# Loosening two waits and regrouping ScalarE's and VectorE's steps between the gMLP layer and the attention layer

## What is computed

```python
y = gmlp_mixer(rms_norm_2(h, a_pre_g[i]), a_w_in[i], ..., a_w_out[i])   # ends in: return y @ w_out
h = h + rms_norm_2(y, a_post_g[i])
kv_in = rms_norm_2(h, kv_norm_g)
k_shared = (kv_in @ w_k).reshape(...)
v_shared = (kv_in @ w_v).reshape(...)
...
y = swa_mixer(rms_norm_2(h, b_pre_g[j]), k_shared, v_shared, b_w_in[j], b_sinks[j], b_w_out[j])
```

## Time and profile before

| | us |
|---|---|
| median of three runs | 874.07 |
| lowest, highest | 873.93, 875.82 |
| the profiled execution | 875.82 |
| its span in the trace | 874.1 |

### The profile page before, as it was taken

How to read it: one execution, slowest core, us unless ns; L and a number is a source line. 1 busy time by engine, 2 the same in 40 slices (tenths; PEclk the granted TensorE clock), 3 DMA queues, 4 the chain that set the end, 5 groups by cost and what they waited for, 6 DMA issues and landing times.

```text
span 874.1 us, 11938 instructions
## 1 busy us (share of the span) xinstructions
PE 862.1 (99%) x4196; PEld 717.8 (82%) x4196; DVE 571.8 (65%) x924; ACT 389.1 (45%) x834; POOL 487.3 (56%) x544
## 2 busy tenths in 40 slices
PE   8999999999999999999999999999999999999997
PEld 6888888888888788888888888888878888888875
DVE  6125647865997589676766535556987477798624
ACT  4123433423666377555112321112787447667622
POOL 7766555682217922318975048771224997566362
PEclk9999999999999999999999999999999999999999
DMA  7543222453971468994742253525963222112202
GB/s 200 168 122 97 73 75 71 130 132 76 224 233 49 141 147 179 219 230 147 173 116 94 82 184 99 127 88 144 229 156 99 73 96 74 49 49 73 73 1 96
DMA packets 83691, 106.84 MB, mean 122 GB/s; under 512 B 11953, under 2 KB 54449, under 8 KB 83634
## 3 DMA queue, kind: packets, MB, share of 16 engines
q1 hardware_dynamic: 72752, 85.12, 30.5%
q0 software_dynamic: 10880, 20.97, 14.2%
q10 hardware_dynamic: 2, 0.00, 0.0%
HBM read 103.98 MB, written 2.10 MB: 121 GB/s over the span
## 4 chain that ended last, share of the span: by engine, by line
PE 90%; POOL 2%; DMA 2%; ACT 2%; issue 2%; DVE 1%; DVEq 0%; POOLq 0%; SPq 0%; ACTq 0%
PE bank L2221 27%; PE bank L2222 27%; PE bank L2223 27%; PE bank L2465 2%; PE bank L2318 1%; PE bank L2493 1%; PE bank L2438 1%; DMA smC<-in_w_v 1%; POOL wlo L880 1%; PE bank L2488 1%; PE bank L2487 1%; POOL ms L830 1%; DMA raw<-in_a_w_out 1%; DVE wlo L1692 1%; ACT junk L980 1%
## 5 line engine op out<-in xcount | busy, mean ns | idle before, releaser
L880 POOL TENSOR_TENSOR wlo<-raw,whi 128x512 fp32r<-128x512 f32 x180 | 247.6, 1407 | 6.3 <-PE bank L2318 5.2
L871 POOL TENSOR_SCALAR whi<-raw 128x512 fp32r<-128x512 f32 x174 | 123.9, 752 | 168.5 <-PE bank L2223 161.1
L2221 PE MATMUL bank<-actB_hi,whi 128*128 128x512 f32 (+1 forms) x416 | 159.6, 384 | 0.1
L2222 PE MATMUL bank<-actB_lo,whi 128*128 128x512 f32 (+1 forms) x416 | 158.6, 381 | 0.0
L2223 PE MATMUL bank<-actB_hi,wlo 128*128 128x512 f32 (+1 forms) x416 | 158.5, 381 | 0.0
L2221 PE MATMUL bank<-whi,actA_hi 128*128 128x512 f32 x350 | 138.2, 395 | 1.2 <-DVE actA_lo L1517 0.7
L2223 PE MATMUL bank<-whi,actA_lo 128*128 128x512 f32 x350 | 136.4, 390 | 0.0
L2222 PE MATMUL bank<-wlo,actA_hi 128*128 128x512 f32 x350 | 136.3, 389 | 0.0
L2223 PEld LDWEIGHTS bank<-actB_hi,wlo 128*128 128x128 f32 x416 | 78.2, 188 | 15.2
L2221 PEld LDWEIGHTS bank<-actB_hi,whi 128*128 128x128 f32 x416 | 78.3, 188 | 15.1 <-issue 0.6
L2222 PEld LDWEIGHTS bank<-actB_lo,whi 128*128 128x128 f32 x416 | 78.3, 188 | 14.0
(11 more groups left out here) (275 smaller groups left out, 1639.3 us busy)
## 6 DMA issues: line engine op xcount, KB each, us to landing
raw<-in_a_w_in SPq DMA_DIRECT2D x44, 512.0 KB, 4.0
raw<-in_w_in SPq DMA_DIRECT2D x32, 512.0 KB, 3.9
raw<-in_b_w_in SPq DMA_DIRECT2D x16, 512.0 KB, 3.4
raw<-in_a_w_out SPq DMA_DIRECT2D x12, 512.0 KB, 3.5
gain<-in_a_w_out POOLq DMA_DIRECT2D x9, 512.0 KB, 9.3
raw<-in_w_ple_gate SPq DMA_DIRECT2D x8, 512.0 KB, 5.1
gain<-in_a_w_in POOLq DMA_DIRECT2D x8, 512.0 KB, 7.1
raw<-in_a_w_in POOLq DMA_DIRECT2D x8, 512.0 KB, 7.4
```

Source lines behind the costliest of these rows:

```text
L871: pool.tensor_scalar(H, src[:, i * HALF:(i + 1) * HALF], 1.0, 1.0, ALU.mult, ALU.mult).then_inc(w_hi, 1)
L880: ins = pool.tensor_tensor(L, src[:, i * HALF:(i + 1) * HALF], H.bitcast(f32), ALU.subtract)
L2221: M(out_, whi_, xhi_, start=start, stop=False)
L2222: M(out_, whi_, xlo_, start=False, stop=False)
```

## The change

It has no new instructions and takes none away. It drops two waits, and it moves steps on ScalarE and VectorE:

```diff
@@ add_a, on POOL
-                    if n == 13:
-                        pool.wait_ge(raw_in[10 + h], LANDED[UNIT_NO["v5", 0], h])
@@ ScalarE
             scale_two("v5", 0)
             hi_a(10)
+            scale_two("v5", 1)
             hi_a(11)
-            scale_two("v5", 1)
             square_a(2, 1)
...
             hi_a(13, (1,))
+            scale_two("k5", 1)
             h3_out(0)
-            scale_two("k5", 1)
             normed_n(0)
-            hi_k5(0)
             h3_out(1)
             turned_n(0)
             normed_n(1)
             square_a(2, 0)
+            hi_k5(0)
             turned_n(1)
+            square_a(3, 0)
             hi_k5(1)
-            square_a(3, 0)
             h3_out(2)
@@ h3_in, on VectorE
-                if t % 2:
-                    dve.wait_ge(rstd_ready["h3"], t)
@@ VectorE
             part_gain(0, 1)
+            lo_a(13, (0,))
             h3_in(0)
-            for h in range(2):
-                lo_a(13, (h,))
             part_gain(1, 1)
+            lo_a(13, (1,))
             h3_in(1)
...
             lo_two(UNIT_NO["v5", 0], 1)
-            lo_two(UNIT_NO["k5", 0], 0)
             add_kept(6, 1, p03_kept(1), a_out_(3, 0), (c7_made, 42 + 10))
             rest_n(1)
             part_gain(2, 0)
             h3_in(2)
-            lo_two(UNIT_NO["k5", 0], 1)
+            for h in range(2):
+                lo_two(UNIT_NO["k5", 0], h)
             part_gain(3, 0)
             h3_in(3)
```

## The result

The changed kernel takes **878.78 us** (median of 4 executions, 878.43 to 879.38) against 874.05 us before: a ratio of **1.0054, 95% interval 1.0041 to 1.0068**. It is slower by 4.7 us, where the forecast was 874.2 us with a range up to 876.7. The profiled execution, one more than these four, took 878.94 us with a span of 877.2 us.

The account below looks back on a forecast made before the run. TensorE, busy without a break after 680 us, was taken as the bound, with 2.66 us idle ahead. Terms 0 + 0 + 0.55 - 0.94 + 0.7 - 0.15, about +0.15 us on the 874.07 median, gave 874.2 us; range 872.5 to 876.7.

Parts of the forecast that it names:

- part 3: Tile 0 of n: k5's scaling ahead of the squares and VectorE's new order make it 0.55 us later.
- row of 0.84 us: Earlier trace row of a POOL step beside an h3_in, taken as the length of tile 0's held root step.
- part 2: ScalarE scales v5's second half before a11's high halves: price 0, with about 1.0 us of cover.
- cover of v5's landing: VectorE is busy until 642.23, hiding about 1.0 us of a11's delay unless v5's second half lands after 639.5.
- Part 1: POOL's a13 adding loads no longer wait for v5, issuing near 630.0 and 631.2: worth 0, price 0.
- would have to share from about 636 us: v5's second half shares with a13's loads only for its last estimated 0.1 MB, taking 1.7 us, landing at 637 to 639.
- row of 1.86 us: Earlier trace row of tile 0's POOL step at 655.24, which took 0.29 us with VectorE silent.
- Part 6: Tiles 2 and 3: tile 2's root waits until about 671.3; the chain releasing 679.03 comes out at 679.2.
- rival b: VectorE starves POOL: tile 0's root passes only after the v5 half, +1.6 us in all, 875.7 us; chance 0.15.
- Parts 4 to 6: Tile 1, k5, then tiles 2 and 3: terms of -0.94, +0.7 and -0.15 us in the sum.
- part 4: Tile 1: k5's high half moves away on ScalarE, 0.94 us less; turn and two v5 products 0.4 us earlier.
- Rival a: POOL's a13 loads share with v5, whose first half lands 2.9 us later, delaying the 638.93 restart: 877.1 us; chance 0.17.

Follow-up runs that it names:

- before_parts_1_2: Kernel before, with POOL's wait for v5 removed and v5's second unit scaled ahead of a11 on ScalarE: 876.82 us.
- after_h3_wait: Changed kernel with VectorE's wait for the previous h3 root put back in h3_in of tiles 1 and 3: 876.13 us.
- after_h3_v5_back: Changed kernel with VectorE's wait for the previous h3 root put back and a11 again ahead of v5's second scaling on ScalarE: 874.00 us.
- before_v5_first: Kernel before, with only v5's second scaling moved ahead of a11 on ScalarE: 875.50 us.
- before_again: Kernel before, unchanged, run again for a second trace: 874.08 us.
- before_no_pool_wait: Kernel before, with only POOL's wait for v5 ahead of a13's adding loads removed: 874.00 us.
- before_a13_split: Kernel before, with a13's weight halves on VectorE placed before h3_in(0) and h3_in(1), and no wait for the previous h3 root: 876.96 us.
- before_no_h3_wait: Kernel before, with only VectorE's wait for the previous h3 root ahead of h3_in(1) and h3_in(3) removed: 875.47 us.
- after_pool_wait: Changed kernel with POOL's a13 loads waiting for v5 again: 877.61 us.
- after_v5_back: Changed kernel with a11's high halves again ahead of v5's second scaling on ScalarE: 876.90 us.

## Why the prediction was wrong

The forecast was no change, and 4.7 us were lost. Two steps failed: in part 3 the price of the hold on tile 0's root (one row of 0.84 us, where the step took 2.19), and in part 2 the cover of v5's landing (637 to 639, where it came at 640.1). The clock, which no term stood for, came on top.

**Part 1, adding loads earlier (0).** Right that v5's first unit isn't slowed: it landed 4.9 us after its issue, at 630.3, before a13's loads (issued at 630.17) could matter. In before_parts_1_2 it was still under way when they were issued at 630.34, and took 8.1 us, no longer than the 8.5 before. The part costs 0.0 us alone. Wrong was the second unit at 637 to 639. It came at 640.1, since SP's queue got 0.00 to 0.16 MB in each 2 us from 630 on. The step that failed is "would have to share from about 636 us": the sharing began at 630, with nearly all of the unit still to come.

**Part 2, v5's scaling ahead of a11 (0, cover 1.0 us).** The failed step is the cover. The limit that was named (a landing after 639.5) was right for the restart at a11 (none in after_h3_wait, landing 639.5; 0.38 us in the changed kernel, 640.1). The landing put against it was 1.1 us or more too early, and it was judged from an execution in which the unit came at 637.1. The reason for the limit was that execution's as well: there VectorE was busy until 642.23, in the changed kernel it stood idle 3.69 us, and so the restart at a13's second half (0.44 and 0.46 us) and a later tile 0 came with it, even at 639.5. Cost beside part 1: 876.82 - 874.19 = 2.6 us; taken out of the changed kernel: 1.9.

**Part 3, tile 0 (+0.55).** The largest miss. The sum took the row of 0.84 us for the root's first step, "the same pair of neighbours", and that step took 2.19, to the end of v5's low part. The row is one of the root's second step (line 833), which takes 0.55 us undisturbed, so the hold in it is 0.3 us. The row of 1.86 us is the one of the right step, and it had already shown a hold that lasted past one boundary. Part 6 of the same prediction priced tile 2's root as held until VectorE's two k5 halves end, and so it came (first step 672.55 to 673.90, the halves to 673.81). The prediction had the long hold at tile 0 as its upper bound and as rival b, at 0.15, and the rows came out as b had them, about 0.6 us later (POOL at 657.46 for 656.86, v5's low part to 659.56 for 659.05). Rival b's price of 1.6 us was too small as well: alone the part costs 2.9 us, with the clock in it and with the missing wait at tile 3.

**The clock.** No term of the sum stood for it. The prediction had counted waits of TensorE only as waits. A wait of 2.8 us was followed by some 3 us at the lower level, 0.9 us net.

**Parts 4 to 6 (-0.94, +0.7, -0.15).** Their sum of -0.4 us can't be told from nothing, and nothing is what the runs show: 0.05 us alone for part 4, 0.2 for k5's scaling, and the whole rest level with before in after_h3_v5_back. VectorE's two k5 halves side by side were never run alone. The gain of part 4 was taken back, as said, though in the kernel before it went at the second v5 product and not at k5's.

**Rival a (877.1)** came near the number by another way. Its mechanism, POOL's queued loads sharing instead of standing in line, is what the second unit shows; for the first unit it was wrong, and the stall it feared, at a10, vanished instead.

**The base.** The differences were taken from one execution that was 1.75 us above the median, and its two restarts (0.43 and 0.65 us) were treated as the kernel's own. They weren't. The one of 0.43 us stands in no other trace. The one at tile 0's turn stands in before_v5_first (0.56) and before_parts_1_2 (0.68), where v5's first unit was late as well (7.6 and 8.1 us to land), and not in before_again or before_no_pool_wait, where it took 4.8 and 4.6. The changed kernel's traces show no idle TensorE before 640 us, yet that gained nothing against the median. Differences from a slow execution don't go onto the median as they are: between the two profiled executions the loss is 3.1 us, between the medians 4.7.

The parts don't simply add: alone or in pairs they cost 2.6 + 2.9 + 0.6 = 6.1 us, together 4.7 to 5.1. The 0.6 us of parts 4 and 5 are within the noise and not seen in after_h3_v5_back, and in the trace of before_parts_1_2 v5's first unit was late besides. Between traces with an early first unit the account closes: about 2.3 and 2.3 us at the turn (4.3 together) and 1.0 for the clock, against the 5.1 measured there.

## What to carry to other kernels

A wait that looks idle may be the only moment in which a neighbour engine gets at the memory; before it is removed, look for small POOL instructions on the path that were long wherever VectorE ran without a pause. Compare each with its own undisturbed time, and price it at the end of the whole run, not at the next boundary. When a transfer is the cover of a reordering, look at its landing in more than one execution: an order that waits for the later of two things is safe only against the latest landing seen. Long waits of TensorE have to be priced with the clock behind them.

## What the runs showed of the hardware

A POOL instruction on 128x1 operands took 0.29 to 0.30 us when VectorE stood still, 0.30 us too beside a VectorE addition with one operand in PSUM (651.93 in the changed kernel), and up to 2.29 (first step) and 2.05 us (second step, otherwise 0.56) beside VectorE instructions with both inputs in SBUF, in a run. It got through at a boundary within a run in before_a13_split (655.98) and before_no_h3_wait (657.24), and at none of two in the five traces with the changed order (2.18 to 2.29 us). The Trainium skill, page "SBUF — State Buffer", section "SBUF: two separate sides", names the exclusion; who comes next in such a run it leaves open, and these rows show that it is mostly VectorE.

The same v5 load, the second unit, took 8.2 to 8.5 us to land where POOL issued a13's first adding load 8.9 to 10.1 us after a12's (before, before_v5_first, before_no_h3_wait, before_a13_split), 9.6 us where it was 6.6 us after (after_pool_wait), and 11.4 to 12.3 us where it was 5.0 to 5.8 us after (the other 13 traces). The first unit took 7.3 to 8.5 us where SP issued it 0.9 to 1.2 us behind POOL's load of a12 (five traces, before among them) and 4.6 to 5.6 us where it was 0.2 to 0.5 us behind (13 traces); no run varied that distance alone, so this is a pattern and not a cause shown. In before_parts_1_2 the first unit was late and the second as well (12.2 us), so it is a13's early issue and not an early first unit that goes with a late second one. TensorE's level fell to 1.2 GHz behind a wait of 2.80 us in both traces of the changed kernel and behind ones of 1.90 us in before_a13_split and 1.89 us in after_pool_wait, but not behind one of 1.89 us in after_v5_back; what tells the last from the other two stays open.
